# Seventh square summed on TensorE, y y sums a tile late, and a four-block opening of the first attention

## The chip, the cores and the metric

The kernel runs on one core of a Trainium2 chip. A core has TensorE (PE) for matmuls, VectorE (DVE), ScalarE (ACT) and GpSimd (POOL) for element-wise work, and DMA queues that are filled by SyncE (SP), ScalarE or GpSimd. The engines run beside each other and wait on semaphores. The metric is device time in microseconds (us), the median of several runs; lower is better.

## The reference, cut to what matters

`x` is [512 tokens, 1024]. The first block is a feed-forward (SwiGLU), a token mixer (mLSTM and HGRN2 heads) and a second feed-forward; then come two layers of attention, a convolutional feed-forward and a gate. Every part has a norm ahead of it and one behind it:

```python
y = rmsnorm(h, ffn1_pre_g[l]) * (1.0 + sc1) + sh1
y = swiglu(y, ffn1_w_gate[l], ffn1_w_up[l], ffn1_w_down[l])
h = h + FFN_RESIDUAL_WEIGHT * g1 * rmsnorm(y, ffn1_post_g[l])
...
for i in range(DEPTH_2):
    g = norm_g[i]
    h = rms_norm(x, g[0])
    ...
    x = x + rms_norm(m, g[1])
    f = conv_glu_ffn(rms_norm(x, g[2]), ffn_w_in[i], ffn_conv_w[i], ffn_conv_b[i], ffn_w_out[i])
    x = x + rms_norm(f, g[3])
    gate = jax.nn.sigmoid(rms_norm(x, g[4]) @ ple_w_gate[i])
    x = x + gate * (p[i] @ ple_w_proj[i])
```

`rms_norm(x, g)` is `x * rsqrt(mean(x * x) + EPS) * g`, the mean over the 1024 features.

## The kernel before, in words

**Tiling.** Activations lie feature-major: `h` is 8 k tiles of 128 features x 512 tokens. A weight block is 128 output features x 8 k tiles. Two neighbouring blocks are a unit, one DMA of 1 MB into one of two `raw` buffers. ScalarE makes the high part of a block (`split_hi`, L743, instruction at L755), VectorE the low part (`split_lo`, L1306, L1311), into one of four places of `wh` and `wl`; each block is multiplied in three passes (`passes`, L1998, instruction at L2002): high x high, low x high, high x low. `gemm` (L2005) does a block of 8 k tiles in 24 matmuls. SyncE may load unit n (L573 to L580) once VectorE has split both blocks of unit n - 2. `split_hi` and `split_lo` run four blocks ahead of TensorE.

**The norms.** They are numbered by `e`, 0 to 15. Seven are post norms: e = 1, 5, 9 and 14 behind the feed-forward blocks (`ffn`), 3, 7 and 12 behind the output products (`product`) of the mixer and the two attentions. Around a post norm, each of the last eight output tiles goes like this: ScalarE squares it from PSUM into one of two `C2` places (`square`, L757, L761), scales and evicts it (L815), and squares the scaled tile (the "y y", L823). VectorE multiplies it with `h` (the "h y", L1352) and adds both to sums (L1358, L1362). GpSimd adds the squares into `acc` (`add_squares`, L619, L632 and L634), seven of the eight. TensorE sums over the partitions by multiplying with ones: `stat_most` (L2055), called two k tiles before the end of the last block, takes `acc`; `stat_last` (L2061) takes the eighth square, the h y sums and the y y sums. ScalarE then makes the reciprocal root (`root`, L773, L770 and L771), VectorE updates `h` (`post`, L1390, or `post_full`, L1373), and `join_sums` (L1364) works out the next norm's mean square from the sums. In the products e = 3, 7, 12 the first four blocks are finished close together, so ScalarE and VectorE work through a backlog; there the y y of tile k waits for VectorE's sum of tile k - 1 (L819).

**The openings.** The first blocks behind a norm are multiplied k tile by k tile, as each k tile of the normed input becomes ready (`opening`, L2018). ScalarE makes its high part (`y_of_h`, L800, L804), VectorE the low part (`low_of_h`, L1332, L1337). In `qkv_first` (TensorE L2304, VectorE L1744) three blocks are done so; the fourth is a `gemm` behind it, and its `split_lo` stands behind `post(5, ...)` at L1930. Then TensorE turns the root into a column (L2300) and goes on with token-major blocks (L2034), whose first PSUM bank must have been evicted by VectorE (L1730), which stands behind `split_lo` of blocks 4, 5 and 6 (L1747).

**Queues.** GpSimd's program is in order: for each post norm `add_squares`, and between them, at e = 2, eight DMAs that write a skewed copy of a bias table to DRAM (rpb_skew, L691) and one of 4 MB that writes another (t_skew, L694), which the attentions read much later. SyncE's queue holds the weight loads. The units of `mix` come from `w_in`, whose rows are 4104 floats long.

Of the kernel before, what the change touches and what calls it, by code (L numbers as in the profile page):

```python
# [15 lines left out]
ALU = mybir.AluOpType  # L16
# [5 lines left out]
KT = D // P  # L22
# [30 lines left out]
POST = [NORMS[:e].count("post") for e in range(len(NORMS))]  # L53
# [29 lines left out]
def build(nc, A, out):  # L83
    ctx = ExitStack()
    with ctx:
# [378 lines left out]
        def evicted(eng, g):  # L464

            eng.wait_ge(gfree[BANK[g]], ORD[g] + 1)
# [74 lines left out]
        def by_row(ap):  # L541

            return ap.rearrange("p (c r) -> p r c", r=8)
# [69 lines left out]
        def _(pool):  # L613
# [73 lines left out]
            for e, norm in enumerate(NORMS):  # L687
                if e == 2:
                    pool.wait_ge(rpb_out, 256)
                    for i in range(8):  # L690
                        pool.dma_start(skew_dram[:, i, :], rpb_dram.rearrange("h q r c -> (h q) (r c)"))\  # L691
                            .then_inc(rpb_skew_out, 16)
                    pool.wait_ge(rows_out, 16)
                    pool.dma_start(rows_skew, rows_dram.rearrange("h (a s) -> h a s", a=1)  # L694
                                   .broadcast_to([8, P, BIAS_ROW])).then_inc(rows_skew_out, 16)
                if e == 3:
                    for n in range(NH * TT):
                        pool.wait_ge(wexp, n + 1)
                        w = C2[:, n % 2, 0:P]
                        nc.gpsimd.affine_select(out=w, in_=w, compare_op=ALU.is_ge, fill=0.0, base=0,  # L700
                                                pattern=[[1, P]], channel_multiplier=-1).then_inc(wdiag, 1)
                if e == 7:
                    na_bands()
                if e == 12:
                    da_bands()
                if norm == "post":
                    add_squares(e, KT - 1)
                elif e == 11:
                    add_squares(e, KT)

# [2 lines left out]
        def _(act):  # L713
# [91 lines left out]
                if e == 11:  # L805
                    square(e, k, h[:, k, :])

            def out_tile(e, k, b, g, yo):

                act.wait_ge(done, b + 1)  # L810
                square(e, k, PS[BANK[g]][:, :])
                to, of = yo[:, k, :], PS[BANK[g]][:, :]
                if e == 7:
                    to, of = rows_of(to), by_row(of)
                nc.scalar.activation(to, of, ACT.Identity, scale=post_scale(e)[:, k:k + 1])\  # L815
                    .then_inc(gfree[BANK[g]], 1)
                evicted(act, g)
                if 2 <= k < KT - 1:
                    act.wait_ge(sums_acc, (KT - 2) * POST[e] + k - 1)  # L819
                if k == KT - 1:  # L820
                    act.wait_ge(most_mm, POST[e] + 1)
                to = acc_yy if k == 0 else A2[:, 1, :] if k < KT - 1 else acc[:, :]
                nc.scalar.activation(to, yo[:, k, :], ACT.Square, scale=1.0 / 32.0).then_inc(yy_ready, 1)  # L823
# [48 lines left out]
            def product(name, e, yo):  # L872
                for b in range(8):
                    if b < 7:
                        split_hi(BB[name] + b + 4)
                    out_tile(e, b, BB[name] + b, TB[name] + b, yo)
                root(e)
                split_hi(BB[name] + 7 + 4)

            def head_square(x):  # L880
# [355 lines left out]
        def _(dve):  # L1236
# [104 lines left out]
                st.do(nc.vector.tensor_tensor(yo[:, k, :], yo[:, k, :], R[:, :], ALU.mult))  # L1341
                st.do(nc.vector.tensor_tensor(h[:, k, :], h[:, k, :], yo[:, k, :], ALU.add))

            def sum_tile(e, k, g, yo):

                p = POST[e]
                evicted(dve, g)
                if k == KT - 1:
                    dve.wait_ge(sq_acc, SQ[e] + KT - 1)
                to = acc_hy if k == 0 else A2[:, 0, :] if k < KT - 1 else C2[:, 0, :]  # L1350
                st.wait()
                hy = nc.vector.scalar_tensor_tensor(to, h[:, k, :], 1.0 / D, yo[:, k, :], ALU.mult, ALU.mult)  # L1352
                if k == KT - 1:
                    hy.then_inc(hy_last, 1)
                    return
                st.do(hy)
                if k:
                    st.step(nc.vector.tensor_tensor(acc_hy, acc_hy, A2[:, 0, :], ALU.add))  # L1358
                    dve.wait_ge(yy_ready, KT * p + k + 1)
                    if k > 1:  # L1360
                        dve.wait_ge(sums_acc, (KT - 2) * p + k - 1)
                    nc.vector.tensor_tensor(acc_yy, acc_yy, A2[:, 1, :], ALU.add).then_inc(sums_acc, 1)  # L1362

            def join_sums(e):  # L1364
                dve.wait_ge(sums_mm, POST[e] + 1)
# [352 lines left out]
            def product(name, e, yo):  # L1718
                for b in range(8):
                    if b < 7:  # L1720
                        split_lo(BB[name] + b + 4)
                    sum_tile(e, b, TB[name] + b, yo)

            def qkv_rooted(layer, x):

# [201 lines left out]
            product("mixo", 3, yo_mix)  # L1927
            post_full(3, yo_mix, BB["ffn1"] + 3)
            ffn(1, 4)
            post(5, yo_ffn)  # L1930
            split_lo(BB["qkv0"] + 3)
            e = 6
            for layer in range(2):
                if layer == 0:
# [15 lines left out]
        def _(pe):  # L1950
# [102 lines left out]
                yield  # L2053

            def stat_most(e):  # L2055
                n = SQ[e] + KT - 1
                pe.wait_ge(sq_acc, n)
                nc.tensor.matmul(X[0][:, :], ones[:, :], by_row(acc[:, :]) if e == 7 else acc[:, :],
                                 start=True, stop=False).then_inc(most_mm, 1)

            def stat_last(e):  # L2061
                n, p = SQ[e] + KT - 1, POST[e]
                pe.wait_ge(sums_acc, (KT - 2) * (p + 1))
                nc.tensor.matmul(X[2][:, :], ones[:, :], acc_hy, start=True, stop=False)
                pe.wait_ge(sq_ready, n + 1)
                c = C2[:, n % 2, :]
                nc.tensor.matmul(X[0][:, :], ones[:, :], by_row(c) if e == 7 else c, start=False, stop=True)\
                    .then_inc(sq_acc, 1)
                nc.tensor.matmul(X[3][:, :], ones[:, :], acc_yy, start=True, stop=False)
                pe.wait_ge(hy_last, p + 1)  # L2070
                nc.tensor.matmul(X[2][:, :], ones[:, :], C2[:, 0, :], start=False, stop=True)
                pe.wait_ge(yy_ready, KT * (p + 1))
                nc.tensor.matmul(X[3][:, :], ones[:, :], acc[:, :], start=False, stop=True).then_inc(sums_mm, 1)
# [230 lines left out]
            def qkv_first(layer, e):  # L2304

                b0, g0 = BB[f"qkv{layer}"], TB[f"qkv{layer}"]
                opening(b0, g0, e, 3, yh, yl)
                gemm(b0 + 3, g0 + 3, yh, yl, middle=(lambda: stat_late(e)) if e == 11 else None, at=2)
                pe.wait_ge(rstd_ready, e + 1)
                root_column()  # L2310
                token_major(b0 + 4, g0 + 4, 0, yh, yl)
                if layer == 0:
                    evicted(pe, g0 + 2)
                    evicted(pe, g0 + 3)
                    na_masks()
                token_major(b0 + 5, g0 + 5, 1, yh, yl)
# [307 lines left out]
```

## Time and profile before

| | before |
|---|---|
| median of 3 runs | 2628.2 us (2627.2 to 2630.8) |
| profiled execution, device time | 2626.46 us |
| its span | 2624.7 us |
| PE / DVE / ACT / POOL busy | 95% / 58% / 38% / 6% |
| granted TensorE clock, mean | 0.984 |

The profiled execution took 1.8 us more than its span, which counts from the first to the last instruction. PE is TensorE's matmuls, PEld its weight loads; a matmul's end is modelled, so the starts are what to compare. The releaser of a wait is inferred from semaphores.

### The profile page before, as it was taken

The numbers are of one execution on the slowest core, as the hardware profiler recorded it, in microseconds if no ns is written. First come the engines' busy times: TensorE is split into PE (matmuls) and PEld (weight loads), VectorE is DVE, ScalarE is ACT, GpSimd is POOL, SyncE is SP. The second block draws the span as 40 slices with busy tenths as digits, with TensorE's granted clock in tenths as the row PEclk, the third lists the DMA queues.
The fourth block names the chain that finished last, engine by engine and source line by source line (L and its number), as shares of the span: only waits on it lengthen the run. The fifth ranks groups of instructions, "written<-read, shape, count | busy, mean of one in ns | idle before, by whom it ended". The sixth has DMA issues, their size and how long they took to land.

```text
span 2624.7 us, 29015 instructions
## 1 busy us (share of the span) xinstructions
PE 2501.1 (95%) x11474; PEld 1973.3 (75%) x11474; DVE 1514.3 (58%) x2363; ACT 999.1 (38%) x1531; POOL 154.3 (6%) x166
## 2 busy tenths in 40 slices
PE   7999998989987999998999999999999999999998
PEld 4878876867766888886877688887776667888876
DVE  5876436667647333336654855534856668555445
ACT  4222234344445333233444433333535554333333
POOL 0000111000010000010101000010100010000100
PEclk9999999999999999999999999999999999999999
DMA  9556428522212333222321222222232212222321
GB/s 363 173 192 199 136 93 151 108 51 52 61 42 67 111 98 99 89 89 72 105 72 59 95 96 97 93 96 93 81 102 70 79 34 95 97 97 93 102 87 64
DMA packets 233703, 265.89 MB, mean 101 GB/s; under 512 B 8376, under 2 KB 222008, under 8 KB 233568
## 3 DMA queue, kind: packets, MB, share of 16 engines
q1 hardware_dynamic: 220704, 223.39, 28.2%
q0 software_dynamic: 11088, 37.46, 4.5%
q10 hardware_dynamic: 1776, 3.18, 0.4%
q8 instruction: 91, 1.49, 0.2%
q14 instruction: 44, 0.36, 0.0%
HBM read 259.78 MB, written 10.75 MB: 103 GB/s over the span
## 4 chain that ended last, share of the span: by engine, by line
PE 62%; DVE 6%; issue 3%; ACT 3%; POOL 0%; DMA 0%; POOLq 0%; ACTq 0%; DVEq 0%
PE G L2002 54%; PE X L2435 1%; DVE wl L1311 1%; PE X L2002 1%; PE G L2454 1%; ACT yh L804 1%; DVE yl L1337 1%; DVE h L1400 1%; PE G L2395 1%; PE X L2362 1%; PE X L2443 1%; DVE tmpA L1352 1%; ACT wh L755 0%; PE X L2376 0%; DVE nbias L1779 0%
## 5 line engine op out<-in xcount | busy, mean ns | idle before, releaser
L1311 DVE TENSOR_TENSOR wl<-raw,wh 128x1024 fp32r<-128x1024 f32 (+1 forms) x398 | 474.7, 1199 | 693.4 <-ACT wh L755 693.1
L2002 PE MATMUL G<-yh,wh 128*128 128x512 f32 x1864 | 755.5, 405 | 49.2 <-DVE yl L1329 15.7
L2002 PE MATMUL G<-yl,wh 128*128 128x512 f32 x1864 | 733.5, 393 | 0.0
L2002 PE MATMUL G<-yh,wl 128*128 128x512 f32 x1864 | 732.8, 393 | 0.0
L755 ACT ACTIVATE wh<-raw 128x1024 fp32r<-128x1024 f32 (+1 forms) x398 | 410.0, 1037 | 815.7 <-PE G L2002 795.7
L2002 PEld LDWEIGHTS G<-yh,wh 128*128 128x128 f32 x1864 | 354.3, 190 | 158.1 <-issue 39.4
L2002 PEld LDWEIGHTS G<-yl,wh 128*128 128x128 f32 x1864 | 353.8, 190 | 76.1
L2002 PEld LDWEIGHTS G<-yh,wl 128*128 128x128 f32 x1864 | 354.7, 190 | 71.8 <-issue 2.7
L2002 PE MATMUL G<-hidh,wh 128*128 128x512 f32 x704 | 279.7, 397 | 0.0
L2002 PE MATMUL G<-hidl,wh 128*128 128x512 f32 x704 | 278.0, 395 | 0.0
L2002 PE MATMUL G<-hidh,wl 128*128 128x512 f32 x704 | 278.0, 395 | 0.0
L2002 PEld LDWEIGHTS G<-hidh,wh 128*128 128x128 f32 x704 | 132.2, 188 | 32.7 <-issue 1.0
L2002 PEld LDWEIGHTS G<-hidh,wl 128*128 128x128 f32 x704 | 132.2, 188 | 32.6 <-issue 1.0
L2002 PEld LDWEIGHTS G<-hidl,wh 128*128 128x128 f32 x704 | 132.2, 188 | 31.9
L634 POOL TENSOR_TENSOR acc<-acc,tmpC 128x512 f32<-128x512 f32 x51 | 86.3, 1691 | 953.4 <-ACT tmpC L761 953.4
L849 ACT ACTIVATE hidh<-tmpA 128x512 fp32r<-128x512 f32 x88 | 55.6, 632 | 214.4 <-DVE tmpA L1455 214.4
L2002 PE MATMUL G<-wh,yh 128*128 128x256 f32 x384 | 114.2, 298 | 3.6 <-DVE mqk L1517 2.0
L2002 PE MATMUL G<-wl,yh 128*128 128x256 f32 x384 | 109.8, 286 | 0.0
L2002 PE MATMUL G<-wh,yl 128*128 128x256 f32 x384 | 109.7, 286 | 0.0
L1458 DVE TENSOR_TENSOR hidl<-tmpA,hidh 128x512 fp32r<-128x512 f32 x88 | 61.0, 693 | 61.5 <-ACT hidh L849 61.5
L2002 PEld LDWEIGHTS G<-wh,yh 128*128 128x128 f32 x384 | 74.7, 194 | 12.1 <-issue 10.1
L1840 DVE CUSTOM_DVE_ANT_0 pb<-X,dbias 128x512 f32<-128x512 f32 x64 | 41.6, 689 | 62.2 <-PE X L2443 55.7
(343 smaller groups left out, 2997.8 us busy)
## 6 DMA issues: line engine op xcount, KB each, us to landing
raw<-in_ffn_w_in SPq DMA_DIRECT2D x44, 1024.0 KB, 5.1
raw<-in_ffn_w_gate SPq DMA_DIRECT2D x22, 1024.0 KB, 5.3
raw<-in_ffn_w_up SPq DMA_DIRECT2D x22, 1024.0 KB, 5.1
ada_c<-in_ada_w POOLq DMA_DIRECT2D x20, 1024.0 KB, 5.6
raw<-in_ffn_w_down SPq DMA_DIRECT2D x16, 1024.0 KB, 5.0
raw<-in_w_in SPq DMA_DIRECT2D x16, 1024.0 KB, 9.2
raw<-in_ffn_w_out SPq DMA_DIRECT2D x16, 1024.0 KB, 5.1
ada_z<-in_ada_w SPq DMA_DIRECT2D x14, 1024.0 KB, 10.9
```

The lines of the kernel that those rows point to most:

```text
L634: nc.gpsimd.tensor_tensor(acc[:, :], acc[:, :], C2[:, n % 2, :], ALU.add)\
L755: nc.scalar.activation(place(wh), src, ACT.Copy).then_inc(hi, 1)
L804: nc.scalar.activation(to, of, ACT.Identity, scale=pre_scale(e)[0][:, k:k + 1]).then_inc(yh_ready, 1)
L849: nc.scalar.activation(hidh[:, 2 * j + i, :], A2[:, i, :], ACT.Copy).then_inc(hidh_ready, 1)
L1311: nc.vector.tensor_tensor(place(wl), src, f32(place(wh)), ALU.subtract).then_inc(lo, 1)
L1337: nc.vector.scalar_tensor_tensor(to, of, pre_scale(e)[0][:, k:k + 1], upper, ALU.mult, ALU.subtract)\
L1352: hy = nc.vector.scalar_tensor_tensor(to, h[:, k, :], 1.0 / D, yo[:, k, :], ALU.mult, ALU.mult)
L1400: nc.vector.tensor_tensor(h[:, k, :], h[:, k, :], yo[:, k, :], ALU.add).then_inc(h_ready, 1)
L1458: nc.vector.tensor_tensor(hidl[:, 2 * j + i, :], A2[:, i, :], f32(hidh[:, 2 * j + i, :]), ALU.subtract).then_inc(hid_ready, 1)
L1840: nc.vector.tensor_tensor_reduce(out=pb[:, c, :], in0=X[m][:, :], in1=dbias[:, x % 2, at:at + S], scale=1.0, scalar=3.0e38, op0=ALU.add, o ...
L2002: ins = nc.tensor.matmul(bank, a, b, start=first and i == 0, stop=last and i == 2)
L2362: nc.tensor.matmul(X[m][:, UC * i:UC * i + w], aq[r, p, qt * P:(qt + 1) * P], ak[r, p, k0:k0 + w], start=True, stop=True).then_inc(na_s, 1)
```

## The change

In the post norms GpSimd adds six squares instead of seven, and TensorE sums the seventh itself at the head of `stat_last`, before the eighth. `stat_most` waits for six. In the three products the y y of a tile is squared by ScalarE one tile later, and those of the last two tiles behind `root`; VectorE adds the y y of tile k - 1 with tile k, that of the seventh tile after the h y of the eighth. In layer 0 the opening of the attention takes four blocks k tile by k tile, and `split_lo` of the fourth moves into `post`, behind its first k tile.

```diff
@@ GpSimd
                 if norm == "post":
-                    add_squares(e, KT - 1)
+                    add_squares(e, KT - 2)
@@ ScalarE
-            def out_tile(e, k, b, g, yo):
+            def out_tile(e, k, b, g, yo, now=True):
...
+                if now:
+                    yy_tile(e, k, g, yo)
+
+            def yy_tile(e, k, g, yo):
                 evicted(act, g)
                 if 2 <= k < KT - 1:
                     act.wait_ge(sums_acc, (KT - 2) * POST[e] + k - 1)
...
                 for b in range(8):
                     if b < 7:
                         split_hi(BB[name] + b + 4)
-                    out_tile(e, b, BB[name] + b, TB[name] + b, yo)
+                    out_tile(e, b, BB[name] + b, TB[name] + b, yo, now=False)
+                    if 1 <= b < 7:
+                        yy_tile(e, b - 1, TB[name] + b - 1, yo)
                 root(e)
+                for b in (6, 7):
+                    yy_tile(e, b, TB[name] + b, yo)
                 split_hi(BB[name] + 7 + 4)
@@ VectorE
+                def add_yy(k):
+                    dve.wait_ge(yy_ready, KT * p + k + 1)
+                    if k > 1:
+                        dve.wait_ge(sums_acc, (KT - 2) * p + k - 1)
+                    nc.vector.tensor_tensor(acc_yy, acc_yy, A2[:, 1, :], ALU.add).then_inc(sums_acc, 1)
...
+                if now and 0 < k < KT - 1:
+                    add_yy(k)
+                if not now and k > 1:
+                    add_yy(k - 1)
...
-                    sum_tile(e, b, TB[name] + b, yo)
+                    sum_tile(e, b, TB[name] + b, yo, now=False)
...
-            post(5, yo_ffn)
-            split_lo(BB["qkv0"] + 3)
+            post(5, yo_ffn, BB["qkv0"] + 3)
@@ TensorE
             def stat_most(e):
-                n = SQ[e] + KT - 1
-                pe.wait_ge(sq_acc, n)
+                pe.wait_ge(sq_acc, SQ[e] + KT - 2)
...
             def stat_last(e):
-                n, p = SQ[e] + KT - 1, POST[e]
+                p = POST[e]
+                for k in (KT - 2, KT - 1):
+                    n = SQ[e] + k
+                    pe.wait_ge(sq_ready, n + 1)
+                    c = C2[:, n % 2, :]
+                    nc.tensor.matmul(X[0][:, :], ones[:, :], by_row(c) if e == 7 else c, start=False, stop=k == KT - 1)\
+                        .then_inc(sq_acc, 1)
                 pe.wait_ge(sums_acc, (KT - 2) * (p + 1))
                 nc.tensor.matmul(X[2][:, :], ones[:, :], acc_hy, start=True, stop=False)
-                pe.wait_ge(sq_ready, n + 1)
-                c = C2[:, n % 2, :]
-                nc.tensor.matmul(X[0][:, :], ones[:, :], by_row(c) if e == 7 else c, start=False, stop=True)\
-                    .then_inc(sq_acc, 1)
...
-                opening(b0, g0, e, 3, yh, yl)
-                gemm(b0 + 3, g0 + 3, yh, yl, middle=(lambda: stat_late(e)) if e == 11 else None, at=2)
+                opening(b0, g0, e, 3 if layer else 4, yh, yl)
+                if layer:
+                    gemm(b0 + 3, g0 + 3, yh, yl, middle=lambda: stat_late(e), at=2)
```

## Rows read from the trace of the kernel before

**Rows 1.** The page's first part: busy time of each engine, whole span.
```profile
PE 2501.1 (95%) x11474; PEld 1973.3 (75%) x11474; DVE 1514.3 (58%) x2363; ACT 999.1 (38%) x1531; POOL 154.3 (6%) x166
```
**Rows 2.** Chain of waits at e = 14: start, length, what, how many.
```profile
2556.43 15.16 PE G L2002 x66
```
**Rows 3.** Timeline, e = 5: start, length, engine, line, operation [idle before, its releaser].
```profile
1186.48 0.40 PE L2002 MATMUL G<-hidl,wh 128*128 128x512 f32 x1
1187.68 1.12 PE L2058 MATMUL X<-acc,ones 128*128 128x512 f32 x2 [0.80 <-POOL acc L634]
...
1190.23 0.60 ACT L761 ACTIVATE tmpC<-G 128x512 f32<-128x512 f32 x1 [3.27 <-PE G L2002]
1191.84 1.02 PE L2069 MATMUL X<-tmpB,ones 128*128 128x512 f32 x2
1192.04 0.69 ACT L770 ACTIVATE rstd<-X,lamc 128x512 f32<-128x512 f32 x1
1192.70 1.02 PE L2071 MATMUL X<-tmpC,ones 128*128 128x512 f32 x2
```
**Rows 4.** Timeline of the product at e = 3: VectorE, TensorE and ScalarE.
```profile
790.59 1.79 DVE L1362 TENSOR_TENSOR tmpB<-tmpB,tmpA 128x512 f32<-128x512 f32 x1
...
804.34 1.12 PE L2058 MATMUL X<-acc,ones 128*128 128x512 f32 x2 [1.67 <-POOL acc L634]
...
806.89 0.60 ACT L761 ACTIVATE tmpC<-G 128x512 f32<-128x512 f32 x1 [1.33 <-PE G L2002]
807.22 0.69 DVE L1362 TENSOR_TENSOR tmpB<-tmpB,tmpA 128x512 f32<-128x512 f32 x1
807.96 1.13 PE L2064 MATMUL X<-tmpB,ones 128*128 128x512 f32 x2 [1.10 <-DVE tmpB L1362]
809.98 0.69 ACT L770 ACTIVATE rstd<-X,lamc 128x512 f32<-128x512 f32 x1 [1.24 <-PE X L2067]
```
**Rows 5.** Timeline of the product at e = 7: TensorE and ScalarE.
```profile
1452.57 2.08 PE L2058 MATMUL X<-acc,ones 128*128 128x512 f32 x2 [1.76 <-POOL acc L634]
...
1460.29 0.69 ACT L770 ACTIVATE rstd<-X,lamc 128x512 f32<-128x512 f32 x1 [1.21 <-PE X L2067]
```
**Rows 6.** Opening of the first attention: timeline, and one piece of the chain (DMA).
```profile
1218.07 1.15 DVE L1337 SCALAR_TENSOR_TENSOR yl<-h,vec,yh 128x512 fp32r<-128x512 f32 x1 [1.39 <-ACT yh L804]
1219.27 0.50 PE L2002 MATMUL G<-yh,wh 128*128 128x512 f32 x1 [0.80 <-DVE yl L1337]
1223.29 5.29 DMA raw<-in_na_w_qkv
...
1231.66 0.36 PE L2002 MATMUL G<-wh,yh 128*128 128x256 f32 x1 [1.64 <-DVE aq L1730]
```
**Rows 7.** Timeline at e = 1, 395 to 431 us: GpSimd, SyncE and ScalarE.
```profile
399.13 1.86 POOL L634 TENSOR_TENSOR acc<-acc,tmpC 128x512 f32<-128x512 f32 x1 [2.35 <-ACT tmpC L761]
410.53 0.37 SPq L580 DMA_DIRECT2D raw<-in_w_in  x1
424.00 1.06 ACT L755 ACTIVATE wh<-raw 128x1024 fp32r<-128x1024 f32 x1 [3.13 <-PE G L2002]
426.15 0.63 ACT L823 ACTIVATE tmpA<-yo_ffn 128x512 f32<-128x512 f32 x1
427.39 4.47 POOL L691 DMA_DIRECT2D rpb_skew<-rpb_rows  x8
430.05 0.60 ACT L761 ACTIVATE tmpC<-G 128x512 f32<-128x512 f32 x1 [3.26 <-PE G L2002]
```
**Rows 8.** DMA issues, us to landing: loads issued at 410.53, 422.2 and 440.4.
```profile
raw<-in_w_in SPq DMA_DIRECT2D x1, 1024.0 KB, 12.3
...
raw<-in_w_in SPq DMA_DIRECT2D x1, 1024.0 KB, 14.6
...
raw<-in_w_in SPq DMA_DIRECT2D x1, 1024.0 KB, 27.5
```
**Rows 9.** Timeline of ScalarE early in mix: the split of block 8.
```profile
482.52 2.01 ACT L755 ACTIVATE wh<-raw 128x1024 fp32r<-128x1024 f32 x2 [1.22 <-DMA raw<-in_w_in]
```

More of the change, by code:

```diff
@@ L1342, in residual, with sum_tile @@
                 st.do(nc.vector.tensor_tensor(h[:, k, :], h[:, k, :], yo[:, k, :], ALU.add))
-            def sum_tile(e, k, g, yo):
+            def sum_tile(e, k, g, yo, now=True):
                 p = POST[e]
+                def add_yy(k):
[3 more added lines that the diff above has]
+                    nc.vector.tensor_tensor(acc_yy, acc_yy, A2[:, 1, :], ALU.add).then_inc(sums_acc, 1)
                 evicted(dve, g)
@@ L1354, in sum_tile @@
                     hy.then_inc(hy_last, 1)
[L1355 to L1362, printed above, removed]
+                else:
+                    st.do(hy)
+                    if k:
+                        st.step(nc.vector.tensor_tensor(acc_hy, acc_hy, A2[:, 0, :], ALU.add))
+                if now and 0 < k < KT - 1:
+                    add_yy(k)
+                if not now and k > 1:
+                    add_yy(k - 1)
             def join_sums(e):
```

## The prediction

> **What bounds the kernel now.** Start with the page: TensorE is busy for 95% of the span, and its granted clock is near full [rows 1]. Where nothing is waited for, a matmul of 512 columns takes 15.16 / 66 = 0.23 us [rows 2]. A change can win only where TensorE stands still, or where it does work that could lie in such a stand. So the next view is the timeline around each of the seven post norms, where the chain of waits leaves TensorE. I call them by the value of `e`: 1, 5, 9 and 14 close a feed-forward block, 3, 7 and 12 close a `product`. In each the same thing is to be seen: in the last block TensorE stops ahead of `stat_most` (L2058), for GpSimd's sum of the seventh square. Behind it stands a second chain: last square, its sum on TensorE, `root`, then VectorE. Last come the openings, where VectorE and ScalarE hand over one k tile at a time and TensorE waits for each, and the DMA queue around the first norm.
>
> **1. The sum of the seventh square.** At e = 5 the gap between matmul starts ahead of L2058 is 1187.68 - 1186.48 = 1.20 us [rows 3]; less the normal 0.23, 0.97 is lost. After the change `stat_most` needs only the sixth square, summed a tile earlier, so the 0.97 goes. The added matmul costs 1192.70 - 1191.84 = 0.86 [rows 3]. It stands at the head of `stat_last`, where the sum of h y stood, while ScalarE squares the eighth tile; so `root` comes 0.97 earlier, and the 0.86 is paid behind it, on the sums that `join_sums` reads. What happens to 0.97:
> e = 5: whole, since `join_sums` comes after all tiles. **-0.97**.
> e = 9, 14: TensorE goes from `stat_last` straight into the projection and is never idle for 15.16 us [rows 2]. Its end of `stat_last` moves by 0.86 - 0.97 = -0.11. **-0.11 each**.
> e = 1: see part 4.
>
> **2. The products (3, 7, 12).** Here TensorE waits longer: 1.67 us at e = 3 ahead of L2058, and 1.10 ahead of L2064 for VectorE's last y y sum [rows 4]. VectorE is late because a sum of it that meets a GpSimd addition takes 1.79 us and not 0.69 [rows 4]. With the y y a tile late, VectorE need not wait for ScalarE, and one GpSimd addition is gone. The first wait is worth 1.67 + 0.17 (what 0.97 was over its own idle 0.80) = 1.84. The second: from the last square to `root` now takes 809.98 - 806.89 = 3.09 [rows 4], where the feed-forward close takes 1192.04 - 1190.23 = 1.81 [rows 3]; with nothing of VectorE's in front I take 1.81, a gain of 1.28. `root` comes 3.12 earlier. But the seventh y y is now squared behind `root` on ScalarE (0.63, the length of such a square [rows 7]), and VectorE waits for it and adds it ahead of its own wait for `root`. Queued behind that addition are the first `times_root` or `residual`, and so everything: 0.63 + 0.69 + 0.08 of hand-over = +1.40. Net:
> e = 12: **-1.7**.
> e = 3: TensorE's four sums wait for that addition too: 4 x 0.86 + 0.2 = 3.65 behind it, while the two residuals take four VectorE steps, 2.9. `join_sums` is 0.75 later: **-1.0**.
> e = 7: the same stop, 1.76 [rows 5], was followed by TensorE at half clock: from L2058 to `root` 1460.29 - 1452.57 = 7.72 [rows 5], at e = 3 it was 809.98 - 804.34 = 5.64 [rows 4]. Without the stop I give those 2.1 back: -1.7 - 2.1 = **-3.8**.
>
> **3. The fourth block in the opening of layer 0.** TensorE now waits about 0.8 per k tile there [rows 6], in a period of 0.8 + 9 x 0.23 and a little, some 3, set by ScalarE and VectorE in turn. Twelve matmuls take 2.8: the fourth block just fits. Its 24 matmuls after the opening (5.6 us) are gone. On VectorE `split_lo` of that block moves from behind `join_sums` to behind the first k tile: every later tile is 1.15 later. It also frees its raw buffer 25 us earlier, so the load that now starts at 1223.29 and takes 5.29 on the chain [rows 6] is long there. What is late next: the seventh low part ends at 1218.07 + 1.15 = 1219.22 now [rows 6], 1220.37 then; `join_sums` 2.8 to 1223.2; ScalarE, after two splits, takes `root` to 1225.3 and split 6 to 1226.2; VectorE split 6 to 1227.5, then the first scaling, 0.7, which frees bank 0 at 1228.2. Now the token-major block starts at 1231.66 [rows 6]. **-3.4**, the 0.97 of part 1 not counted again. TensorE idles some 5 us ahead of it and may fall to 1.2 GHz; it already does in the first token-major block, so I price that at nothing, 1.7 at most.
>
> **4. What moves on GpSimd's queue at e = 1.** One addition fewer is not all. Behind `add_squares(1)` stand eight issues of rpb_skew, which take 4.47 us, and one of t_skew, the 4 MB that L694 writes. They now wait for the seventh square and go from 427.39 on, t_skew from 431.9 [rows 7]. The sixth addition ends at 399.13 + 1.86 = 401.0, so they go 26 us earlier: into the end of the first feed-forward block. There SyncE issues the load of mix's second unit at 410.53 [rows 7], which lands 12.3 us later [rows 8], at 422.8, and ScalarE splits it at 424.00 [rows 7]: 1.2 us of slack. The same kind of load issued at 440.4, 8 us behind t_skew, takes 27.5 [rows 8]. ScalarE's split stands ahead of the squares of tiles 7 and 8. The price lies between 12.3 (no contention: nothing) and 27.5. I take 26, close to the contended row, since its place behind t_skew is alike, and a little under since this load alone is the quick one. It lands at 436.5; ScalarE does split, square, eviction and y y in 2.8 and squares the eighth tile at 439.3 instead of 430.05 [rows 7]. So e = 1 is not -0.97 but **+9.3**; it hides nothing, since TensorE is long done with the block. Given back: the load for block 8 of mix, for which ScalarE waited 1.22 [rows 9] while t_skew ran, is free: **-1.2** (0 to 1.2).
> The Trainium skill (DMA: Bandwidth & Descriptors, Queues, rings and completion order) says that each DMA engine goes round between the queues that have work, packet by packet. By an even share 12.3 would become 24.6, the landing 435.1 and the term +7.9; the sum below would end 1.4 lower.
>
> **The sum.** +9.3 - 1.2 - 1.0 (e = 3) - 0.97 - 3.4 - 3.8 - 0.11 - 1.7 - 0.11 = -3.0. The profiled execution took 2626.46 for a span of 2624.7, 1.7 below the median of 2628.2; every term is small against both, so I take it off the median: **2625.2**.
>
> **Rivals.**
> A. *The transfers do not meet* (or the late split is hidden): e = 1 is -0.97 and the -1.2 falls away. Sum -12.1: 2616.1. For it: the load issued 5 us ahead of the transfers took 14.6 [rows 8], hardly more than 12.3. Against it: in the new place they have nine us of start.
> B. *Slower: the seventh y y behind `root` decides.* If VectorE stays the last in the products (GpSimd's additions now fall on its longer operations, so it doesn't catch up), the 3.12 are not won while the 1.40 are paid. It decides when VectorE's last h y sum ends later than TensorE's last block. The products then give +1.4 + 2.1 + 1.4 instead of -6.5, sum +8.4: 2636.6.
> C. *Slower: the meeting is worse.* The load waits for its forerunner as well, which is now in flight with the first skews; ten us more: 2635.2.
> D. *The fourth block brings nothing* (split 6, or a clock fallen in the longer gap, takes the 3.4): 2628.6, no change.
>
> **How the numbers follow.** Forecast 0.53, with 2620 to 2631 as its own range (landing from 23 to 29 us after issue: -2.6 and +2.6; parts 2 and 3 to 3 either way). A 0.20, B 0.09, C 0.08, D 0.10. A measurement of this kernel can tell about 0.2%, 5.3 us, from no change. Below 2622.9 lie A and a third of the forecast: 0.38. Above 2633.5 lie B, C and the edge of the forecast: 0.18. Between: 0.44. The range runs from 2614.5 to 2633.5: it takes in A and D and leaves out B and C.
>
> **What would show it.** L2058 without idle before it at all seven places. At e = 1 GpSimd's DMA issues near 401, a raw load near 27 us, ScalarE idle ahead of its third split of mix, and TensorE idle ahead of `stat_last` by some 10 us. At 3, 7 and 12 `root` 1.8 behind the last square, and VectorE idle, then one y y sum, ahead of its first product with `root`. At the first attention twelve matmuls per k tile, no wait for a DMA, and the token-major block about 4.4 us nearer to the norm. The prediction is wrong if the load at 410 lands within 14 us (then A), or if TensorE waits for VectorE at the end of the products (then B).

## The result and the profile after

The changed kernel takes **2631.09 us** (median; 2626.16 to 2635.84) against 2626.56 (2619.89 to 2631.05) for the kernel before, measured beside it: a ratio of 1.0018, interval 1.001 to 1.0025. It is slower by 4.5 us where 3.0 less was forecast: the time lies inside the stated range of 2614.5 to 2633.5, but it moved the other way. The profiled execution took 2630.83 for a span of 2629.1, 4.4 more than the span of the kernel before.

TensorE's busy time rose by 7.0 us [rows 1]. The page of the kernel after:

```profile
PE 2508.1 (95%) x11488; PEld 1976.5 (75%) x11488; DVE 1506.5 (57%) x2363; ACT 997.4 (38%) x1531; POOL 142.8 (5%) x159
```

Seven additions fewer on GpSimd, fourteen matmul passes more on TensorE: that is the change of part 1. To see where the time went I took the same instruction in both timelines and subtracted its starts. Where this offset moves, the time of that stretch changed.

| Stretch | Offset at its end | Change | Forecast |
|---|---|---|---|
| up to 420, ahead of the change's first effect | +1.2 | +1.2 | 0 |
| e = 1, to `root` | +12.7 | **+11.5** | +9.3 |
| mix | +11.3 | -1.4 | -1.2 |
| e = 3, to the second root | +11.9 | **+0.5** | -1.0 |
| ffn1 and e = 5 | +10.6 | -1.2 | -1.0 |
| opening, to the first token-major block | +7.6 | -3.1 | -3.4 |
| first attention | +8.2 | +0.6 | 0 |
| e = 7, product to ffn2 | +6.8 | **-1.4** | -3.8 |
| ffn2 and e = 9 | +5.7 | -1.1 | -0.1 |
| second attention | +8.4 | +2.6 | 0 |
| e = 12, product to ffn3 | +6.2 | -2.2 | -1.7 |
| e = 14 and the last stage | +4.4 | -1.8 | -0.1 |

Two of these cuts need a word. The row of e = 9 ends at its `root`; the added sum, 0.86, is paid right behind it (L2069 stands at +6.6). So e = 9 gives 0.2 and 0.9 of the +2.6 in the row below belongs to it; 1.6 more of that row comes in one step between 2113 and 2117. At e = 14 `root` is 1.1 earlier, 0.9 of it comes back behind it, and 1.6 is won in the gate's opening, where matmuls start 0.43 us apart in the kernel before and 0.23 in the changed one: a clock that no edit there accounts for.

**e = 1.** The timeline, GpSimd, then SyncE, TensorE and ScalarE:

```profile
400.31 1.85 POOL L634 TENSOR_TENSOR acc<-acc,tmpC 128x512 f32<-128x512 f32 x1 [2.34 <-ACT tmpC L761]
402.10 4.46 POOL L691 DMA_DIRECT2D rpb_skew<-rpb_rows  x8
406.54 1.10 POOL L694 DMA_DIRECT2D t_skew<-t_rows  x1
...
401.04 11.05 SPq L580 DMA_DIRECT2D raw<-in_w_in  x2
...
440.73 3.80 PE L2082 MATMUL X<-tmpC,ones 128*128 128x512 f32 x4 [10.60 <-ACT tmpC L761]
...
439.13 1.06 ACT L755 ACTIVATE wh<-raw 128x1024 fp32r<-128x1024 f32 x1 [17.08 <-DMA raw<-in_w_in]
...
441.82 0.58 ACT L761 ACTIVATE tmpC<-G 128x512 f32<-128x512 f32 x1
...
444.56 0.69 ACT L770 ACTIVATE rstd<-X,lamc 128x512 f32<-128x512 f32 x1 [0.92 <-PE X L2082]
```

The nine skew DMAs go right behind the sixth addition, 25 us earlier than before [rows 7]. The second of the two loads in the SyncE row is issued at 411.7; the DMA view of 411 to 413 gives its landing:

```profile
raw<-in_w_in SPq DMA_DIRECT2D x1, 1024.0 KB, 27.4
```

It was 12.3 [rows 8]. ScalarE's split waits 17 us for it, the squares of tiles 7 and 8 stand behind that split, and TensorE stands 10.6 us ahead of L2082, the two squares in `stat_last`.

**e = 3.** The timelines of TensorE, ScalarE and VectorE, as [rows 4]:

```profile
820.65 2.08 PE L2085 MATMUL X<-tmpB,ones 128*128 128x512 f32 x2 [2.68 <-DVE tmpB L1361]
822.52 1.80 PE L2086 MATMUL X<-tmpB,ones 128*128 128x512 f32 x2
...
816.19 0.60 ACT L761 ACTIVATE tmpC<-G 128x512 f32<-128x512 f32 x1 [1.55 <-PE G L2017]
...
818.00 0.69 ACT L770 ACTIVATE rstd<-X,lamc 128x512 f32<-128x512 f32 x1 [0.64 <-PE X L2082]
...
819.26 0.61 ACT L827 ACTIVATE tmpA<-yo_mix 128x512 f32<-128x512 f32 x1
...
819.90 0.69 DVE L1361 TENSOR_TENSOR tmpB<-tmpB,tmpA 128x512 f32<-128x512 f32 x1 [1.81 <-ACT tmpA L827]
...
826.14 0.69 DVE L1383 TENSOR_TENSOR acc<-X,rstd 128x512 f32<-128x512 f32 x1 [2.77 <-PE X L2090]
```

`root` comes 1.81 behind the last square, as forecast, and 3.3 earlier. But VectorE waits 1.81 for the seventh y y, squared behind `root`, TensorE stands 2.68 for VectorE's sum, and then runs the sums at a fallen clock. VectorE waits 2.77 more. The same view by stretches, granted clock third from the end:

```profile
818.00:821.00 3.00, 0.35 (x1) 0.35 (x2) 1.19 (x3) 2.97 (x5) 0.00 (x0) 0.94 0.00 0
821.00:825.00 4.00, 4.00 (x6) 1.54 (x6) 2.27 (x4) 0.34 (x1) 0.00 (x0) 0.62 0.00 0
```

0.62 of the full 2.4 GHz over four us: mostly the lower level.

**e = 7.** TensorE, then ScalarE, as [rows 5]:

```profile
1458.92 2.00 PE L2072 MATMUL X<-acc,ones 128*128 128x512 f32 x2
...
1462.14 3.83 PE L2082 MATMUL X<-tmpC,ones 128*128 128x512 f32 x4
1468.65 1.57 PE L2085 MATMUL X<-tmpB,ones 128*128 128x512 f32 x2 [2.69 <-DVE tmpB L1361]
...
1466.00 0.69 ACT L770 ACTIVATE rstd<-X,lamc 128x512 f32<-128x512 f32 x1 [2.49 <-PE X L2082]
```

The stop ahead of `stat_most` is gone, yet its two passes still take 2.00 us, and the four of L2082 take 3.83.

**The opening.** TensorE and VectorE, as [rows 6]:

```profile
1215.41 0.50 PE L2017 MATMUL G<-yh,wh 128*128 128x512 f32 x1 [0.20 <-DVE yl L1345]
...
1238.40 1.28 DVE L1746 SCALAR_TENSOR_TENSOR aq<-G,rstd 128x512 f32<-128x512 f32 x2
```

With twelve matmuls per k tile TensorE waits 0.20, not 0.80.

### The profile page after: what moved, and what is told of

It reads as the page before. It is cut to its first block, busy times and chain, and to the rows that moved or that the text cites. A ratio compares the mean times of both kernels' runs of the same rounds, so it can differ in the third digit from the quotient of the medians.

```text
span 2629.1 us, 29029 instructions
## 1 busy us (share of the span) xinstructions
PE 2508.1 (95%) x11488; PEld 1976.5 (75%) x11488; DVE 1506.5 (57%) x2363; ACT 997.4 (38%) x1531; POOL 142.8 (5%) x159
## 4 chain that ended last, share of the span: by engine, by line
PE 66%; DVE 4%; ACT 2%; issue 1%; DVEq 0%; ACTq 0%
PE G L2017 58%; PE X L2017 1%; PE X L2453 1%; PE G L2472 1%; ACT yh L804 1%; DVE yl L1345 1%; DVE h L1416 1%; PE G L2413 1%; PE X L2380 1%; DVE wl L1319 1%; PE X L2461 1%; PE X L2394 0%; PE X L2082 0%; ACT wh L755 0%; DVE nbias L1795 0%
## 5 line engine op out<-in xcount | busy, mean ns | idle before, releaser
L634 POOL TENSOR_TENSOR acc<-acc,tmpC 128x512 f32<-128x512 f32 x44 | 74.9, 1703 | 849.8 <-ACT tmpC L761 849.8
```

Source lines behind the costliest of these rows:

```text
L634: nc.gpsimd.tensor_tensor(acc[:, :], acc[:, :], C2[:, n % 2, :], ALU.add)\
```

## The experiments

Twelve kernels. A difference in us is taken between the medians of the kernel and of the kernel before beside it.

**e1_skew_back.** Is the loss at e = 1 the place of the DMAs? GpSimd's part gets one wait:

```diff
                 if e == 2:
                     pool.wait_ge(rpb_out, 256)
+                    pool.wait_ge(sq_ready, SQ[1] + KT)
                     for i in range(8):
                         pool.dma_start(skew_dram[:, i, :], ...
```

> The changed kernel with one wait more: GpSimd issues the nine skew DMAs only when ScalarE has squared the eighth tile of e = 1, so they go at about 427 again and not at 402. Nothing else differs. Theory (the early transfers delay the raw load of mix's second unit, and that is the whole of the loss at e = 1): the load issued at about 411 lands in 12 to 13 us and not 27, ScalarE's split of it doesn't wait, root of e = 1 comes 12.7 - 1 = 11.5 to 12.5 us earlier than in the changed kernel, and the 1.2 that block 8 of mix lost to the transfers in the kernel before is lost again. Net 10 to 11 us less than the changed kernel: 6 to 7 us less than the kernel before, ratio about 0.9975. Rival 1 (the load is late for another reason, its own forerunner or the order of SyncE's queue): root of e = 1 stays at 444, ratio 1.0018 as with the changed kernel. Rival 2 (what e = 1 gets back is taken at e = 2 to 5 by transfers that are now late): root of e = 1 at 432 but ratio between 0.999 and 1.001.

Ratio 0.9977, interval 0.9964 to 0.9991: 6.5 us less than the kernel before, 11 less than the changed kernel by the two ratios. The load of 411 lands in 11.9, and ScalarE waits for TensorE, not for it:

```profile
425.43 1.06 ACT L756 ACTIVATE wh<-raw 128x1024 fp32r<-128x1024 f32 x1 [3.13 <-PE G L2018]
...
432.23 0.69 ACT L771 ACTIVATE rstd<-X,lamc 128x512 f32<-128x512 f32 x1
...
484.23 2.01 ACT L756 ACTIVATE wh<-raw 128x1024 fp32r<-128x1024 f32 x2 [2.58 <-DMA raw<-in_w_in]
```

`root` of e = 1 is 12.3 earlier than in the changed kernel, and the wait at block 8 of mix is back, at 2.6. Both rivals fall.

**e2_skew_early_alone.** The other half: the kernel before, with nothing but the DMAs moved.

```diff
+            def skews():
+                pool.wait_ge(rpb_out, 256)
...
             def add_squares(e, count):
                 for k in range(count):
+                    if e == 1 and k == KT - 2:
+                        skews()
```

> The kernel before with one thing moved: GpSimd issues the nine skew DMAs between its sixth and its seventh addition of e = 1, at about 402, where the changed kernel has them; it still adds the seventh square, behind their issue. Theory (collision): the raw load at 411 takes about 27 us, ScalarE's split of it waits about 15 us for it, root of e = 1 is 11.5 to 13 later, the 1.2 at block 8 of mix comes back, net +10 to +12 us, ratio 1.004. Rival (the loss at e = 1 of the changed kernel comes from the seventh square on TensorE or another part of the change): ratio 1.000, root of e = 1 within 1 us of 431.9. The issue of the skews takes 5.6 us on GpSimd and the seventh square is not there before the load has landed, so that the addition behind them costs nothing of its own.

Ratio 1.0058 (1.0037 to 1.0079): 15.8 slower, more than either line gave. The load takes 27.3 and the mechanism is the one expected, but the time is above the 10 to 12 forecast: `root` of e = 1 is 14.9 late, not 12.7. In the timeline of TensorE and in the stretches around it:

```profile
440.91 2.08 PE L2061 MATMUL X<-acc,ones 128*128 128x512 f32 x2 [14.61 <-POOL acc L645]
```

```profile
436.00:440.00 4.00, 0.00 (x0) 0.00 (x0) 1.49 (x2) 2.55 (x4) 0.95 (x1) 0.50 0.74 200
440.00:446.00 6.00, 5.09 (x11) 2.89 (x12) 2.70 (x3) 1.28 (x3) 0.86 (x1) 0.67 0.52 204
```

Here the seventh square still goes over GpSimd, so TensorE stops in the middle of its last block, its granted clock falls to 0.50, the lower level of 1.2 GHz, and the rest of the block is done behind the stop. In the changed kernel the block was finished before the stop. From ScalarE's split to `root` it takes 9.3 here (437.42 to 446.73) and 5.4 there (439.13 to 444.56): the seventh square with TensorE takes 3.9 off the damage.

**e9_rpb_early and e10_t_early.** Which of the transfers does it, eight of 480 KB or the one of 4 MB? Each holds back one kind with the wait of e1.

```diff
e9:
                         pool.dma_start(skew_dram[:, i, :], ...
+                    pool.wait_ge(sq_ready, SQ[1] + KT)
                     pool.wait_ge(rows_out, 16)
                     pool.dma_start(rows_skew, ...
e10:
+                    pool.wait_ge(rows_out, 16)
+                    pool.dma_start(rows_skew, ...
+                    pool.wait_ge(sq_ready, SQ[1] + KT)
                     pool.wait_ge(rpb_out, 256)
                     for i in range(8):
```

> The changed kernel with t_skew's DMA alone held back until ScalarE has squared the eighth tile of e = 1; the eight rpb_skew DMAs (8 x 480 KB) still go at 402. It tells which of the two collides. If every queue with work takes an even share of the engines (so that any of them slows the load alike while it lasts): the load of 412 takes 20 to 27 us. If it is t_skew's 4 MB that delays it: 12 to 14 us and root of e = 1 at about 432 to 433.

> The changed kernel with the eight rpb_skew DMAs held back until ScalarE has squared the eighth tile of e = 1; t_skew's DMA (4 MB) alone goes at 402. Even share: the load takes 20 to 27 us. If it is the 480 KB transfers that delay it: 12 to 14 us.

ScalarE's third split, in e9 and in e10:

```profile
432.16 1.06 ACT L756 ACTIVATE wh<-raw 128x1024 fp32r<-128x1024 f32 x1 [9.97 <-DMA raw<-in_w_in]
```

```profile
434.56 1.06 ACT L756 ACTIVATE wh<-raw 128x1024 fp32r<-128x1024 f32 x1 [12.61 <-DMA raw<-in_w_in]
```

Each kernel was run once: 2624.61 and 2627.45, with 2625.75 for the kernel before. The load takes 20.3 us behind the small transfers, 22.9 behind the large one, 27.4 behind both, 11.9 behind none: both lie in the 20 to 27 expected of an even share, and either kind does it, for as long as it runs. How the engines were shared shows in the DMA view by queue (GpSimd's is q0, SyncE's q1; packets, MB, share of the 16 engines). The changed kernel from 412 to 424, then two parts of it, 412 to 415 and 416 to 424:

```profile
q0 software_dynamic: 679, 2.71, 67.2%
q1 hardware_dynamic: 400, 0.41, 33.6%
...
q0 software_dynamic: 246, 1.10, 101.2%
...
q0 software_dynamic: 348, 1.26, 51.8%
q1 hardware_dynamic: 356, 0.36, 48.3%
```

e10, from 412 to 424:

```profile
q1 hardware_dynamic: 704, 0.72, 60.2%
q0 software_dynamic: 433, 1.77, 35.8%
```

In the kernel before the load had the engines alone from 411 to 422: 1.01 MB, 94%. The 33.6% of the changed kernel is a mean of two stretches. Issued at 411.7, the load moves nothing until 415, while GpSimd's queue has all the engines; alone, in e1, its first packets move 1.1 us behind the issue. From 416 on the two queues have almost equal time. GpSimd's packets, as the profile counts them, are of about 4 KB (2.71 MB / 679), SyncE's of 1.0 KB, so unequal packets don't explain a share below half: they are as unequal from 416 on, and in e10, where SyncE's queue has the larger share. The Trainium skill (DMA: Bandwidth & Descriptors, Queues, rings and completion order) has the engines go round packet by packet. The 348 and 356 packets from 416 to 424 agree, as the profile counts packets; the empty 3 us ahead of them and the 704 against 433 of e10 are not explained by it, and no run here shows their reason. The even share of the prediction, a landing after 24.6, is 2.8 short of the 27.4; the late start is 2.2 longer than in e1 and accounts for most of that, by this estimate from the two traces.

**e3_skew_back_no_defer.** Was the y y a tile late needed? e1 with the products' y y in the order of the kernel before:

```diff
-                    out_tile(e, b, BB[name] + b, TB[name] + b, yo, now=False)
-                    if 1 <= b < 7:
-                        yy_tile(e, b - 1, TB[name] + b - 1, yo)
+                    out_tile(e, b, BB[name] + b, TB[name] + b, yo)
                 root(e)
-                for b in (6, 7):
-                    yy_tile(e, b, TB[name] + b, yo)
...
-                    sum_tile(e, b, TB[name] + b, yo, now=False)
+                    sum_tile(e, b, TB[name] + b, yo)
```

> As e1_skew_back (skews wait for the eighth square), and besides the three products (e = 3, 7, 12) square y and add y y in the order of the kernel before: no tile late, and nothing of y y behind root. The seventh square stays with TensorE everywhere. Theory 1 (VectorE catches up by the missing GpSimd addition alone, and the sum behind root costs 1.4 each): root of the products stays about 3 us earlier than in the kernel before and the 1.0 to 1.4 behind it goes, with the sums of e = 3 back at 3.6 us: 3 to 5 us less than e1_skew_back. Theory 2 (the delay of y y is what lets VectorE catch up): root falls back by 1 to 3 us in each product and the 1.4 is won: between 1.5 less and 4 more than e1_skew_back, and TensorE waits again for VectorE's y y sum ahead of the sums of its last tile.

Ratio 0.9949 (0.9931 to 0.9966): 13.8 less than the kernel before, 7.3 less than e1. Theory 1 has its direction, though the gain is above its 3 to 5. VectorE at e = 3 (L1358 is the y y sum, L1365 the last h y):

```profile
801.23 1.79 DVE L1358 TENSOR_TENSOR tmpB<-tmpB,tmpA 128x512 f32<-128x512 f32 x1
...
805.40 0.69 DVE L1358 TENSOR_TENSOR tmpB<-tmpB,tmpA 128x512 f32<-128x512 f32 x1
...
808.46 0.69 DVE L1358 TENSOR_TENSOR tmpB<-tmpB,tmpA 128x512 f32<-128x512 f32 x1
809.06 0.69 DVE L1365 SCALAR_TENSOR_TENSOR tmpC<-h,yo_mix 128x512 f32<-128x512 f32 x1
```

As long as GpSimd adds squares each y y sum that meets it takes 1.79; the last two meet nothing and take 0.69. The addition that went to TensorE is what lets VectorE catch up: TensorE waits 0.28 for its last sum, where it waited 1.10 [rows 4].

**e6_yy_before_root.** The other way to the same question: e1 with the y y a tile late, but the seventh ahead of `root`.

```diff
+                yy_tile(e, 6, TB[name] + 6, yo)
                 root(e)
-                for b in (6, 7):
-                    yy_tile(e, b, TB[name] + b, yo)
+                yy_tile(e, 7, TB[name] + 7, yo)
```

> As e1_skew_back, with one thing moved in the three products: ScalarE squares the seventh tile's y ahead of root and no longer behind it. Theory (what the changed kernel loses behind root is the sum of that square, for which VectorE waits ahead of its first product with root): root 0.6 later than in e1, the 1.8 idle of VectorE ahead of the y y sum behind root gone, the sums of e = 3 on TensorE back at 3.6 us from 5.5; each product 0.8 and e = 3 up to 3 less than in e1: 2.5 to 4 less in all, close to e3. Rival (the y y a tile late costs by filling VectorE or ScalarE earlier on): as e1, within 1.

Ratio 0.9944 (0.993 to 0.9957): 15.0 less than the kernel before. That is 8.5 less than e1, twice what was expected, and level with e3. VectorE at e = 3:

```profile
808.58 0.68 DVE L1362 TENSOR_TENSOR tmpB<-tmpB,tmpA 128x512 f32<-128x512 f32 x1
809.95 0.69 DVE L1350 TENSOR_TENSOR yo_mix<-yo_mix,rstd 128x512 f32<-128x512 f32 x1 [0.69 <-ACT rstd L772]
...
813.12 0.69 DVE L1384 TENSOR_TENSOR acc<-X,rstd 128x512 f32<-128x512 f32 x1 [0.30 <-PE X L2091]
```

The sum now lies in the time in which VectorE waits for `root` anyway, which still comes 1.81 behind the last square. The 1.81 and the 2.77 of the changed kernel are gone (0.69 and 0.30 here). So it is the place behind `root` that costs, not the delay by a tile.

e6 also shows what is special at e = 7. TensorE there, and its stretches:

```profile
1443.16 2.00 PE L2073 MATMUL X<-acc,ones 128*128 128x512 f32 x2
...
1446.40 3.83 PE L2083 MATMUL X<-tmpC,ones 128*128 128x512 f32 x4
1450.06 1.04 PE L2086 MATMUL X<-tmpB,ones 128*128 128x512 f32 x2
```

```profile
1440.00:1446.00 6.00, 6.00 (x22) 3.78 (x21) 5.93 (x9) 3.27 (x5) 0.00 (x0) 1.00 0.54 178
1446.00:1450.00 4.00, 4.00 (x7) 1.08 (x6) 1.66 (x3) 1.69 (x3) 0.00 (x0) 1.00 0.00 0
```

The clock is full, 1.00, and the sums take 2.00 all the same. What sets L2073 and L2083 apart from the 1.04 of L2086 is in the code: `by_row(acc[:, :]) if e == 7`, an operand read with a step of 8 floats. From L2083 to L2086 four passes take 3.66, 1.83 for each sum, against 0.86 elsewhere.

**e5_square_alone.** Part 1 by itself: six squares for GpSimd, `stat_most` and `stat_last` of the changed kernel, skew DMAs as in e1, all else as before.

```diff
-                    add_squares(e, KT - 1)
+                    add_squares(e, KT - 2)
...
+                for k in (KT - 2, KT - 1):
+                    n = SQ[e] + k
+                    pe.wait_ge(sq_ready, n + 1)
...
```

> The kernel before with one part of the change alone: GpSimd adds six squares, TensorE sums the seventh and the eighth at the head of the last sums; the skew DMAs wait for the eighth square of e = 1 as in e1. No y y a tile late, no four-block opening. Theory (e3 is the kernel before plus this plus the opening, and the parts add up): e3 took 13.8 less than the kernel before and the opening alone 3.4, so this takes about 10 less, ratio 0.996; the last VectorE y y sum of each product takes 0.69 and not 1.78, VectorE is done ahead of TensorE, root of e = 3, 7 and 12 comes 2.5 to 3.5 earlier. Rival (e3 gains by the meeting of parts, such as a clock that didn't fall at e = 7): 5 to 7 less, with the clock fallen at e = 7.

Ratio 0.9952 (0.9938 to 0.9965): 12.7 less, above the 10 expected. With the 3.4 of e4 that makes 16.1, and e3, which has both, has 13.8: the parts don't quite add up. Nearly all that the change can bring is in this part. From the product's first matmul to its `root`, e = 3 is 3.3 shorter than in the kernel before, e = 7 2.5 and e = 12 3.2; another 1.7 lies in the opening that follows e = 5.

**e4_opening_alone.** Part 3 by itself.

```diff
-                opening(b0, g0, e, 3, yh, yl)
-                gemm(b0 + 3, g0 + 3, yh, yl, middle=(lambda: stat_late(e)) if e == 11 else None, at=2)
+                opening(b0, g0, e, 3 if layer else 4, yh, yl)
+                if layer:
+                    gemm(b0 + 3, g0 + 3, yh, yl, middle=lambda: stat_late(e), at=2)
```

> The kernel before with the opening of the first attention alone changed: four blocks k tile by k tile, the fourth block's low part split behind the first k tile, its 24 matmuls behind the opening gone. Theory (the changed trace has the offset of the token-major start fall by 3.07): 3 us less than the kernel before, ratio 0.9989. Rival (what is won there is given back in the next stage by a clock that stays low longer, or by the later split of the first scaled k tiles): 0 to 1 us less, ratio 1.000; the first token-major block then takes over 8 us.

Ratio 0.9985 (0.9973 to 0.9997): 3.4 less, as forecast, though the interval reaches from 0.8 to 7.1. In the profile the stretch itself gains 2.7 (below).

**e7_skew_in_ffn1 and e8_skew_in_ffn1_no_defer.** A better place for the transfers: `if e == 2` becomes `if e == 4`, behind the additions of e = 3. e7 is the changed kernel with that, e8 is e3 with that.

> The changed kernel with the nine skew DMAs issued a stage later, behind GpSimd's additions of e = 3, so in the second feed-forward block. Theory: nothing meets the raw loads of mix, root of e = 1 is 12 earlier than in the changed kernel and the 1.2 at block 8 of mix stays won; in the feed-forward block the raw loads have the slack of whole pairs: 1.2 less than e1_skew_back, 7 to 8 less than the kernel before. Rival (the transfers, some 7.9 MB, meet the loads of ffn1 and make ScalarE wait there, or the biases are late for their reader): as much as 10 lost between e = 3 and e = 5, ratio at or above that of the changed kernel.

> e7 and e3 together: skew DMAs in the second feed-forward block, y y of the products in the old order, seventh square with TensorE, opening of four blocks. If both theories hold this is the best version: 1.2 less than e3, some 15 less than the kernel before, ratio 0.9944. If the transfers meet the loads of ffn1 it is slower than e3 by what e7 is slower than e1.

Ratios 0.9978 (0.9968 to 0.9988) and **0.9941** (0.9927 to 0.9954). GpSimd issues them at 801 in e7, the split at block 8 of mix waits for nothing, and none in ffn1 does:

```profile
800.83 4.46 POOL L691 DMA_DIRECT2D rpb_skew<-rpb_rows  x8
```

```profile
481.49 2.00 ACT L755 ACTIVATE wh<-raw 128x1024 fp32r<-128x1024 f32 x2
```

But the 1.2 that this was to bring against e1 doesn't show: the ratios are 0.9978 and 0.9977, and by the median e7 is only 3.8 less than the kernel before. e8 against e3 is within the intervals. e8 has the lowest ratio of all, 15.9 us less than the kernel before.

**e11_best and e12_best_three_blocks.** e6 and e7 together, and the same with the old opening of three blocks.

> e6 and e7 together: the changed kernel with the skew DMAs behind the additions of e = 3, in the second feed-forward block, and the seventh tile's y squared ahead of root in the products. Theory: e6 took 15.0 less than the kernel before with the skews at the end of e = 1; in e8 against e3 their place in the feed-forward block gave 1 to 2 more. So 16 to 17 less than the kernel before, ratio 0.9938, at or below both kernels and all runs so far. Rival (the y y a tile late itself costs, and e6's gain over e3 is scatter): as e8, 15 less or not as much.

> As e11 with the first attention's opening of the kernel before: three blocks k tile by k tile, the fourth behind them. It tells what the opening of four is worth when the rest of the change is in place. Rival 1 (the parts add up): 3 more than e11, as e4 took 3.4 less than the kernel before. Rival 2 (in the opening of four TensorE stands still in the gaps and its granted clock falls, 0.83 in 1220 to 1240 of e3 and e6 against 1.00 in e5, which has three blocks and the square with TensorE; the kernel before had 0.91 there by its wait ahead of the norm): 0 to 1 more than e11, and with the second scaling of the token-major blocks at most 1 later.

Ratios 0.995 (0.993 to 0.997) and 0.9954 (0.9939 to 0.9968), 14.0 and 12.4 less. e11 doesn't beat e6 or e8: its rival holds, and from e3, e5, e6, e8, e11 and e12 these runs can pick no best. The opening of four is worth 1.6 here by the medians, far inside the intervals, so only its own stretch can tell why that isn't 3.4. 1220 to 1240 in e12 and in e11 (PE busy first, granted clock third from the end):

```profile
1220.00:1240.00 20.00, 18.40 (x135) 16.92 (x134) 9.47 (x19) 5.06 (x8) 0.77 (x2) 1.00 0.39 124
```

```profile
1220.00:1240.00 20.00, 16.42 (x111) 15.78 (x110) 12.20 (x22) 5.59 (x8) 0.00 (x0) 0.83 0.33 106
```

From `root` of e = 5 to VectorE's second scaling of a token-major block e11 gains 2.6 on the kernel before, e12 1.5, e4 2.7 and e5 1.7. With three blocks that stretch gets 1.5 to 1.7 without any edit of its own, at a clock of 1.00 in e5 and e12 where the kernel before had 0.91. With four TensorE stands in front of the token-major block and has 0.83. So the opening adds 1.1 and not 2.7, by one profile of each kernel.

## Why the prediction was wrong, step by step

**The sign hung on three terms, 6.1 us of the 7.4 between the sum, -3.0, and the two profiles, +4.4.** e = 1 cost 2.2 more, e = 3 1.5 more, and e = 7 gained 2.4 less. The other four parts, mix, e = 5, the opening and e = 12, came within 0.5 each and 0.6 lower together. The remaining 1.8 is in stretches for which I had forecast nothing or 0.1: +1.2 ahead of the change, +0.6 and +2.6 in the attentions, less 1.0 and 1.7 at e = 9 and 14. Each offset is of one profile of each kernel; the sign of the whole rests on the medians of 20 runs.

**e = 1: right mechanism, undersized.** The step "a little under since this load alone is the quick one" is the one that failed: 27.4, not 26. The load was the quick one, yet met both kinds of transfer. That is 1.3; the other 0.9 is the clock, which I had not counted: behind a stop of 10.6 L2082 takes 3.80, where it takes 1.97 at e = 3, at a granted clock of 0.50 from 440 to 445. e1 and e2 show that the place of the DMAs is the cause, from both sides; in e9 and e10 either kind alone still delays the load, by 8 and 11 us. Rivals A and C fall with this: the forerunner, issued at 401.0, took 10.0 and had landed before the load was issued.

**e = 7: a wrong reading of a right number.** "Followed by TensorE at half clock" is half of the truth, and "I give those 2.1 back" is the step that failed. The kernel before, TensorE behind the stop, then the stretch 1452 to 1456:

```profile
1455.72 0.63 PE L2002 MATMUL G<-oh,wh 128*128 128x512 f32 x1
...
1457.01 1.41 PE L2064 MATMUL X<-tmpB,ones 128*128 128x512 f32 x2
```

```profile
1452.00:1456.00 4.00, 3.44 (x6) 1.74 (x7) 3.96 (x5) 0.63 (x1) 0.51 (x1) 0.80 0.65 226
```

The 2.1 between [rows 5] and [rows 4] is the net of three things. Two sums by `by_row` are 0.97 longer each: +1.9. Six matmuls of the block run at the lower clock, 0.43 apart and not 0.23: +1.2. And the wait of 1.10 for VectorE, which e = 3 has, isn't there. Only the 1.2 follows from the stop, and it was given back: from L2058 to the last square took 4.67 and now takes 3.42. No stop causes the longer sums and none taken away gives them back; the changed kernel even adds a third. The 2.00 us of L2073 at a clock of 1.00 in e6 shows it. So `root` is 2.5 earlier (stop 1.85, clock 1.25, less 0.6 for the third long sum), and behind `root` 1.1 is lost: -1.4. The forecast had 1.28 of e = 3 in it, for a wait that e = 7 never had, took all of the 2.1 for the clock and charged nothing for the third sum. The code says `if e == 7` in the very line.

**e = 3 (and all products): right gain, wrong price.** "`root` 3.12 earlier" came as 3.3. But "`join_sums` is 0.75 later" assumed that TensorE's four sums run at 0.86 behind the wait. They waited 2.68 and then ran at the lower clock, 5.5 us in place of 3.65. e6, which only moves the seventh square ahead of `root`, takes the loss away. Behind `root` the changed kernel lost 3.9 at e = 3, for 2.15 in the forecast, and 1.1 each at e = 7 and 12, for 1.40. There was no need to pay it: e3 has the gain without the y y a tile late. The step "with the y y a tile late, VectorE need not wait for ScalarE" gave the gain to the wrong edit. It belongs to "one GpSimd addition is gone". Rival B had VectorE take away the 3.12. It didn't, `root` came earlier in every run. But the sign named for it, TensorE waiting for VectorE at the end of the products, did appear: the 2.68, behind `root` and not ahead of it. That sign couldn't tell the two apart.

**The opening: right by itself.** e4 has 3.4 for a forecast of 3.4 by the medians, with an interval wide enough that the closeness is luck; its stretch has 2.7 there and 3.1 in the changed kernel. "I price that at nothing, 1.7 at most", of the clock in the gap, holds only while the clock has fallen there without the opening too. With the other parts in place and the clock otherwise full, it takes 1.6 of the 2.7.

**e = 12** came as -2.2 for -1.7, mix as -1.4 for -1.2.

**What stays open.** Of the +2.6 in the second attention, the 1.6 between 2113 and 2117. From 2100 to 2135 the granted clock is 1.00 in the kernel before, e5, e6, e8 and e11, 0.95 in the changed kernel and 0.85 in e3, and a head's work there takes 19.7, 21.3 and 24.1 us. No edit touches that stretch, and kernels as alike as e11 and e12 differ in it. Nor is it known why e3 and e6 are 7.3 and 8.5 less than e1 by their medians, when the stretches of the products account for 6.1 and 5.8: 3.9 and 3.6 at e = 3 and 1.1 each at e = 7 and 12, the clock of 2100 aside.

## What to carry to other kernels

An instruction taken out of a queue moves all that stands behind it. Here the addition was cheap, and nine DMA issues of 7.9 MB behind it met the one load on the path: pin such transfers with a wait to the event that they are to follow, or put them where loads have slack. When a change bundles edits, price the gain by edit: the one that moves a unit of work to an engine with time (seven matmuls) brought 12.7 of 15, and the reordering that was to help it took 6 to 8 back. Don't conclude a clock from a duration: read the granted clock of the stretch, and look for what is special in that line. And don't carry a difference between two places over as one cause before its parts are counted.

## What the hardware showed

A sum over an operand read with a step of 8 floats takes 1.83 us where the plain one takes 0.86, at the same granted clock of 1.00 (e6, L2083 and L2086). A load issued behind nine transfers moved nothing for 3.3 us, where alone it started after 1.1; then the two queues had 51.8% and 48.3% of the engines (416 to 424), although the packets of one were of 3.6 KB and those of the other of 1.0 KB. The load took 27.4 us behind all nine, 22.9 behind the one of 4 MB, 20.3 behind the eight small ones and 11.9 behind none.
